# Gate projections moved from the merge stage into the stick-breaking heads of a hybrid decoder layer

## The chip, the cores and the metric

The kernel runs on all 8 cores of one Trainium2 chip. Each core computes one of the 8 batch entries, with no exchange between cores. The metric is the time on the device of the slowest core, in microseconds (us). Engines: PE is the matrix engine (TensorE), DVE VectorE, ACT ScalarE, POOL GpSimd, SP the engine that only issues DMAs here.

## The reference

One decoder layer for x of 2048 tokens by 2048 channels per core. A token mixer (two kinds of attention side by side, 8 heads of 128 each) and a SwiGLU follow one another, each between RMS norms.

```python
u = rms_norm(x)
q_sb,k_sb,v_sb, q_fx,k_fx,v_fx, f_logit, g_sb, g_fx = split(u @ w_in)     # g_*: 2048 columns each
# stick-breaking head: z = q k^T / sqrt(128), strictly causal (s < t)
#   w[t,s] = sigmoid(z_ts) * prod_{s<j<t} (1 - sigmoid(z_tj));   o = w v
# forgetting (fox) head: softmax of z + c[t] - c[s], c = cumulative log sigmoid(f_logit), s <= t
merged = sigmoid(g_sb) * (o_sb @ w_branch_sb) + sigmoid(g_fx) * (o_fx @ w_branch_fox)
h   = x + rms_norm(merged @ w_out)
out = h + rms_norm(swiglu(rms_norm(h)))                                   # d_ff = 5632
```

## The kernel before

Everything is held transposed: channels (or head dimensions) on the 128 partitions, tokens along the free axis. A matmul has 128x128 weights (bf16) and up to 512 token columns. D = 2048 gives KC = 16 channel tiles; the 2048 tokens are NCH = 4 chunks of 512, or two halves of TH = 1024. Weights lie in memory as float32.

The kernel writes a list of instructions for each engine (`KB.op`, `KB.group`, `KB.dma`) and waits between engines come from the buffers that each operation reads and writes. Every engine runs its list in order, so the order in which the Python code emits the work is the order of execution. All compute operations have line 83 in the profile, that of the replay; the tile names tell them apart.

**Front.** x is loaded twice in 16 tiles of 128 x 2048 float32 through two buffers `xs`. The first pass squares each tile on ACT and sums over channels by matmuls with ones (`sq`); `rstd_from_banks` (L362) makes 1/rms by Ln and Exp on ACT. The second pass scales each tile on DVE into `uT` (bf16, the normed input, kept in SBUF). `stage2` (L402) computes the forget logits and the bias tables of the fox heads. Then q, k and v of head 0 are projected.

**Heads.** The 8 stick-breaking heads run first, then the 8 fox heads. While head i runs, the projections of head i+1 run beside it: `head_filler` (L679) makes 24 items of 8 matmuls each (`proj_items`, L484: for each token chunk k, q, v in two halves), and `Filler.tick` emits them evenly over the head's own work. Weights of head i+2 are loaded by SP as float32 (`wst`) and cast on DVE to `wbf` (`load_head`, L463). A finished projection is moved from PSUM by DVE: q and k by a scaled copy, v by a copy into `VT` and a DMA transpose on SP.

`attn_sb` (L597) takes 16 rows of 128 queries, in 24 pieces of up to 1024 keys: logits on PE, `filler.tick`, two sigmoids on ACT (`kap`, `bet`), masks by POOL, a running product (scan) and a product on DVE, then a DMA transpose of the weights on SP into `WTA` or `WTB`. The logits use two pairs of PSUM banks, so piece g+2 waits for the sigmoids of piece g. The value matmuls of a chunk (`pv`, L643) are emitted later: `Steps` is a planner that counts nominal time (`HEAD_US` = 57 us a head) and emits deferred work when its due time has come, here 8 us after the chunk's last piece.

`attn_fox` (L704) takes 40 blocks of 128 keys by 512 queries: logits on PE, `filler.tick`, Exp on ACT into one of 6 buffers `p`, mask on POOL for diagonal blocks, the sum of p on DVE (`acc`), value matmuls 2.7 nominal us later. At the end of a chunk `finish_chunk` (L746) splits the sum into two bf16 parts, adds up over partitions on PE, takes a reciprocal on DVE and multiplies. Each head's output goes to DRAM (`OTs`) through SP.

**Merge.** `P5` (L903) runs once for each half of the tokens. It loads the outputs of all 16 heads (`OTh`, 4 MB) and then, for each of 16 column tiles c, three weight tiles (two gates and the branch weights, float32 by SP, cast by DVE), and computes per 512 tokens 16 + 16 gate matmuls on `uT` and 8 + 8 branch matmuls on `OTh`:

```python
kb.op(ACT, "activation", dict(out=a1.t[:, :], in_=bset[0][0][:, :], func=AF.Sigmoid), ...)
kb.op(DVE, "tensor_tensor", dict(out=m1.t[:, :], in0=bset[2][0][:, :], in1=a1.t[:, :], op=ALU.mult), ...)
kb.op(POOL, "tensor_tensor", dict(out=merged.t[:, c, hsl], in0=m1.t[:, :], in1=m2.t[:, :], op=ALU.add), ...)
```

`WOUT` (L973) follows each half with the output projection. After that come the second norm and the SwiGLU (`GATEUP`, `DOWN`), whose weights POOL loads with a cast to bf16 on the way.

Of the kernel before, what the change touches and what calls it, by code (L numbers as in the profile page):

```python
# [7 lines left out]
F32 = mybir.dt.float32  # L8
# [5 lines left out]
S = 2048  # L14
# [74 lines left out]
class KB:  # L89
# [156 lines left out]
def build_nc(debug=None, upto=99):  # L246
# [16 lines left out]
    G["OTs"] = nc.dram_tensor("OTs", [2 * NH, DH, S], BF16).ap()  # L263
    G["mixs"] = nc.dram_tensor("mixs", [D, S], F32).ap()
# [42 lines left out]
def _emit(nc, kb, banks, G, upto):  # L307
# [5 lines left out]
    gains_d, bf_d, cbf_d, cf_d, outT = G["gains_d"], G["bf_d"], G["cbf_d"], G["cf_d"], G["outT"]  # L313
    OTs, mixs, hs, ffs, dbg = G["OTs"], G["mixs"], G["hs"], G["ffs"], G["dbg"]
# [33 lines left out]
    pre = Slot(kb, "pre", [128, 136], F32)
    cumL = Slot(kb, "cumL", [128, 128], F32)
# [38 lines left out]
    rstd_from_banks([0, 1, 2, 3], rstd1.t, rstd1.r, 0, tmp)
    for c in range(KC):
        x = xs[c % 2]  # L390
        kb.dma(SP, x.ds, x.t[:, :], xT[c * 128:(c + 1) * 128, :], writes=[x.r])
        kb.op(DVE, "scalar_tensor_tensor", dict(out=uT.t[:, c, :], in0=x.t[:, :], scalar=gains.t[:, c:c + 1],
                                                in1=rstd1.t[:, :], op0=ALU.mult, op1=ALU.mult),
              reads=[x.r, gains.r, rstd1.r], writes=[uT.r])
    dump("rstd1", rstd1.t[:, :], rstd1.r)
    if dbg is not None and "uT" in dbg:
        dump("uT", uT.t[:, :, :], uT.r, dbg["uT"].rearrange("(c p) t -> p c t", p=128))
# [825 lines left out]
```

How the kernel before makes its waits and increments, by code:

```python
    def replay(self, eng):  # L70
        regs = {}
        for it in self.prog:
            if it[0] == "w":
                eng.wait_ge(it[1], it[2])
            else:
                _, calls, sem, inc = it
                ins = None
                for meth, kw in calls:
                    if meth == "affine_select":
                        if kw["fill"] not in regs:
                            regs[kw["fill"]] = eng.to_reg(kw["fill"])
                        kw = dict(kw, fill=regs[kw["fill"]])
                    ins = getattr(eng, meth)(**kw)
                    if inc == 16:
                        ins.then_inc(sem, 16)
                if inc == 1:
                    ins.then_inc(sem, 1)
```

## Time and profile before

| | |
|---|---|
| median of 3 runs | 4568.84 us (4557.34, 4568.84, 4719.97) |
| profiled execution | 4541.18 us |
| span of its slowest core (core 5) | 4539.6 us; others 4505.8 to 4533.7 |
| busy share of the span | PE 85%, DVE 35%, ACT 21%, POOL 16% |
| chain that ended last | PE 69%, DMA 11%, DVE 10%, issue 4%, ACT 3%, POOL 2% |
| bytes moved by DMA | 595 MB, mean 131 GB/s |

All rows are from core 5. Times count from the start of its span. "Busy" PE counts matmuls with modelled ends, so a busy PE need not run at its peak; the count of matmuls in a stretch says more. PEclk is the share of full clock that was granted (1.00 is 2.4 GHz, 0.50 is 1.2 GHz). The idle time of an engine is put down to what ended it (`<-`).

### The profile page before, as it was taken

Reading aid. Unit: us, or ns where it says so; the run is one execution under the profiler, and the core shown is the slowest. Engines: PE = TensorE matmul, PEld = TensorE weight load, DVE = VectorE, ACT = ScalarE, POOL = GpSimd, SP = SyncE. Lnnn points to the kernel's source line nnn. Section 1 sums busy time; section 2 is a strip of 40 time slices with the busy share of each in tenths; the row PEclk is TensorE's granted clock in tenths of the full one; section 3 lists DMA queues with packets and bytes.
Section 4 is the critical chain, followed back from the end, with each engine's and each line's share of the span. In section 5 each row is a group of like instructions: output and inputs, shape, how many; then the busy total and the mean of one; then the engine's idle time right before and its main releaser. Section 6 shows DMA issues by size and latency. Waiting matters only on the chain.

```text
span 4539.6 us, 52571 instructions; the slowest of 8 cores (4505.8 to 4539.6 us)
## 1 busy us (share of the span) xinstructions
PE 3868.3 (85%) x17500; PEld 1709.3 (38%) x17500; DVE 1601.8 (35%) x1822; ACT 942.2 (21%) x1421; POOL 725.1 (16%) x933
## 2 busy tenths in 40 slices
PE   2477777779895999989976699998998999999994
PEld 0232333334341444434432244443444444444431
DVE  1478888877776333123322211111100111110001
ACT  3044444434333111211123011111111000000100
POOL 0022222211111111011123011111000111110113
PEclk9998988999997999999998899999999999998886
DMA  6444444321111443654368655565754666558897
GB/s 225 134 102 101 95 109 102 95 75 54 67 45 60 166 150 121 212 185 156 151 215 256 144 117 118 119 121 100 157 114 89 122 120 121 110 114 155 163 197 192
DMA packets 331515, 595.40 MB, mean 131 GB/s; under 512 B 197616, under 2 KB 206320, under 8 KB 298480
## 3 DMA queue, kind: packets, MB, share of 16 engines
q1 hardware_dynamic: 270320, 363.40, 28.7%
q0 software_dynamic: 42496, 195.06, 21.4%
q10 hardware_dynamic: 18432, 33.56, 2.2%
q8 instruction: 145, 2.38, 0.2%
q14 instruction: 122, 1.00, 0.1%
HBM read 633.86 MB, written 75.50 MB: 156 GB/s over the span
## 4 chain that ended last, share of the span: by engine, by line
PE 69%; DMA 11%; DVE 10%; issue 4%; ACT 3%; POOL 2%; DVEq 0%; SPq 0%; ACTq 0%; POOLq 0%
PE ps L83 69%; DVE Pr_43_85 L83 2%; DVE Pr_44_86 L83 2%; DMA mh_106_148<-mixs 2%; DMA xs_23_65<-xT 1%; DMA WTA_47<-wp_45_87 1%; DMA wd_175_217<-wfd_t 1%; ACT kap_39_81 L83 1%; DVE acc_55_97 L83 1%; DMA fl_186_228<-ffs 1%; DVE rec_59_101 L83 1%; DMA xs_22_64<-xT 1%; DMA hs<-hst_108_150 1%; DMA hl_131_173<-hs 0%; DVE uT_49 L83 0%
## 5 line engine op out<-in xcount | busy, mean ns | idle before, releaser
L83 DVE TENSOR_TENSOR_SCAN Pr_43_85<-kap_39_81 128x640 f32<-128x640 f32 (+4 forms) x96 | 160.0, 1667 | 2.2 <-POOL kap_39_81 L83 1.4
L83 PE MATMUL ps<-uT_49,wbf_1_11_53 128*128 128x512 bf16 x512 | 129.7, 402 | 32.2 <-DVE wbf_1_11_53 L83 18.5
L83 PE MATMUL ps<-u_124_166,wgu_0_143_185 128*128 128x512 bf16 x480 | 109.9, 382 | 52.4 <-DVE u_124_166 L83 52.4
L83 PE MATMUL ps<-uT_49,wbf_1_14_56 128*128 128x512 bf16 x512 | 128.1, 397 | 12.7 <-DVE qT_28_70 L83 8.4
L83 POOL TENSOR_SCALAR_AFFINE_SELECT kap_39_81<-kap_39_81 128x128 f32<-128x128 f32 x96 | 45.8, 477 | 581.9 <-ACT kap_39_81 L83 581.1
L83 PE MATMUL ps<-uT_49,wbf_2_12_54 128*128 128x512 bf16 x512 | 123.5, 386 | 15.7 <-DVE kT_29_71 L83 15.5
L83 DVE TENSOR_SCALAR tmpD_169<-ps 128x512 f32<-128x512 f32 x6 | 4.1, 689 | 372.0 <-PE ps L83 366.8
L83 PE MATMUL ps<-uT_49,wbf_0_13_55 128*128 128x512 bf16 x512 | 133.7, 410 | 1.5 <-DVE Pr_44_86 L83 1.5
L83 PE MATMUL ps<-aT_167,wd_153_195 128*128 128x512 bf16 x528 | 120.1, 389 | 14.4 <-DMA wd_153_195<-wfd_t 14.4
L83 PE MATMUL ps<-uT_49,wbf_0_10_52 128*128 128x512 bf16 x512 | 129.7, 402 | 1.1 <-DVE Pr_44_86 L83 1.0
L83 POOL TENSOR_TENSOR merged_104<-m_102_144,m_103_145 128x512 bf16<-128x512 f32 x32 | 63.7, 1990 | 418.1 <-DVE m_103_145 L83 418.1
L83 PE MATMUL ps<-aT_167,wd_175_217 128*128 128x512 bf16 x484 | 120.6, 415 | 8.7 <-DMA wd_175_217<-wfd_t 8.7
L83 PE MATMUL ps<-uT_49,wbf_2_15_57 128*128 128x512 bf16 x512 | 122.2, 382 | 6.0 <-DVE kT_32_74 L83 5.8
L83 DVE TENSOR_TENSOR aT_167<-ps,sg_174_216 128x512 bf16<-128x512 f32 x44 | 30.4, 691 | 273.5 <-PE ps L83 273.5
L83 DVE TENSOR_TENSOR aT_167<-ps,sg_150_192 128x512 bf16<-128x512 f32 x44 | 30.4, 691 | 272.5 <-PE ps L83 272.5
L83 DVE TENSOR_TENSOR aT_167<-ps,sg_173_215 128x512 bf16<-128x512 f32 x44 | 30.4, 691 | 263.6 <-PE ps L83 263.6
L83 DVE TENSOR_TENSOR aT_167<-ps,sg_149_191 128x512 bf16<-128x512 f32 x44 | 30.4, 691 | 262.6 <-PE ps L83 262.6
L83 PE MATMUL ps<-u_124_166,wgu_0_167_209 128*128 128x512 bf16 x480 | 110.4, 384 | 10.1 <-DMA wgu_0_167_209<-wfg_t 10.1
L83 DVE TENSOR_TENSOR_SCAN Pr_44_86<-kap_40_82,Pr_44_86 128x512 f32<-128x512 f32 (+3 forms) x64 | 116.3, 1818 | 7.2 <-DVE Pr_44_86 L83 0.5
L83 PE MATMUL ps<-aT_167,wd_176_218 128*128 128x512 bf16 x484 | 116.3, 404 | 1.3 <-DMA wd_176_218<-wfd_t 1.3
L83 PE MATMUL ps<-aT_167,wd_177_219 128*128 128x512 bf16 x440 | 111.0, 419 | 7.2 <-DMA wd_177_219<-wfd_t 7.2
L83 POOL TENSOR_TENSOR merged_104<-m_76_118,m_77_119 128x512 bf16<-128x512 f32 x32 | 63.5, 1986 | 305.4 <-DVE m_77_119 L83 305.4
(396 smaller groups left out, 7211.6 us busy)
## 6 DMA issues: line engine op xcount, KB each, us to landing
wst_8_50<-wqkv_t SPq DMA_DIRECT2D x24, 1024.0 KB, 6.0
wst_9_51<-wqkv_t SPq DMA_DIRECT2D x24, 1024.0 KB, 6.2
xs_22_64<-xT SPq DMA_DIRECT2D x16, 1024.0 KB, 5.7
xs_23_65<-xT SPq DMA_DIRECT2D x16, 1024.0 KB, 5.9
wstA_64_106<-wg_t SPq DMA_DIRECT2D x16, 1024.0 KB, 5.9
wstA_65_107<-wg_t SPq DMA_DIRECT2D x16, 1024.0 KB, 6.1
wstA_90_132<-wg_t SPq DMA_DIRECT2D x16, 1024.0 KB, 6.3
wstA_91_133<-wg_t SPq DMA_DIRECT2D x16, 1024.0 KB, 6.2
```

Source lines behind the costliest of these rows:

```text
L83: ins = getattr(eng, meth)(**kw)
```

## The change

1. Fox heads run first, stick-breaking heads last. `HEAD_US` is split into `FOX_US` = 58 and `SB_US` = 107, the planner's times.
2. The gate projections leave `P5`. They become 256 filler items of 8 matmuls beside the stick-breaking heads; ACT applies the sigmoid from PSUM and SP stores the result as float32 in DRAM (`gts`, 16.8 MB). `P5` reads it back (1 MB a column tile) and keeps only the branch matmuls.
3. x is loaded once, by token chunk. Each chunk is squared, summed, scaled and projected for the first head before the next is finished.
4. Weights of heads, gates and branches are loaded by POOL with a cast on the way; the float32 buffers and the DVE casts go.
5. q, k and v are moved from PSUM by ACT. In the fox heads the reciprocal on DVE becomes Ln and Exp on ACT; there are 10 `p` buffers, value matmuls come after 4.3 us, the split after 4.3 and the denominator after 8.

```diff
+    def group(self, E, calls, reads=(), writes=(), part=()):      # part: writes without a wait on the own engine
-            kb.dma(SP, sl.ds, sl.t[:, :, :], wqkv_t[br * 24 + j * 8 + h], writes=[sl.r])
-            kb.op(DVE, "tensor_copy", dict(out=dst.t[:, :, :], in_=sl.t[:, :, :]), reads=[sl.r], writes=[dst.r])
+            kb.dma(POOL, sl.ds, sl.t[:, :, :], wqkv_t[br * 24 + j * 8 + h], reads=after, writes=[sl.r])
...
-                kb.op(DVE, "tensor_scalar", dict(out=o_, in0=bt[:, :], scalar1=sc, scalar2=None, op0=ALU.mult),
+                kb.op(ACT, "activation", dict(out=o_, in_=bt[:, :], func=AF.Copy, scale=sc), writes=[br_, dres[tc]])
-                kb.op(DVE, "tensor_copy", dict(out=o_, in_=bt[:, :]), writes=[br_, vt.r])
+                kb.op(ACT, "activation", dict(out=o_, in_=bt[:, :], func=AF.Copy), writes=[br_, vt.r])
...
+    for tc in range(2):
+        for g in range(4):
+            x_load(tc, g)                                          # SP: 4 channel tiles x 512 tokens, 1 MB
+    for ld in load_head(heads[0], 0, after=[xr[0][1]]):
+        ld()
+    for ld in load_head(heads[1], 1, after=[xr[1][3]]):
+        ld()
+    for g in range(4):
+        x_sq(0, g)                                                 # ACT
+        x_stat(0, g)                                               # PE, 4 matmuls
+    x_norm(0)                                                      # rstd, 16 scalings of 512 on DVE, x_load(tc + 2)
+    for g in range(4):
+        x_sq(1, g)
+    for tc in range(NCH):
+        items = proj_items(heads[0], 0, 0, tcs=[tc])
+        for it in items[0:2]:                                      # k
+            it()
+        if tc + 1 < NCH:
+            for g in range(4):
+                x_stat(tc + 1, g)
+            x_norm(tc + 1)
+        if tc + 2 < NCH:
+            for g in range(4):
+                x_sq(tc + 2, g)
+        forget_logits(tc)
+        if tc + 1 == NCH:
+            forget_bias()
+        for it in items[2:]:                                       # q, v
+            it()
...
-            steps.after(2.7, pvm)
+            steps.after(4.3, pvm)
...
-                kb.op(DVE, "reciprocal", dict(out=rc.t[:, :], in_=bD[:, :]), writes=[rD, rc.r])
+                kb.op(ACT, "activation", dict(out=rc.t[:, :], in_=bD[:, :], func=AF.Ln), writes=[rD, rc.r])
+                kb.op(ACT, "activation", dict(out=rc.t[:, :], in_=rc.t[:, :], func=AF.Exp, scale=-1.0), writes=[rc.r])
...
-            steps.after(4.0, dmm)
+            steps.after(8.0, dmm)
...
+    def gate_load(n):
+        sl = wgt[n % 3]
+        kb.dma(POOL, sl.ds, sl.t[:, :, :], wg_t[n], writes=[sl.r])
+    def gate_items(n):                                             # load of n + 2 goes with the first item
+        wsl = wgt[n % 3]
+        def evict_at(tc):
+            def evict(bt, br_):
+                st_ = gst[cnt["g"] % 3]
+                cnt["g"] += 1
+                kb.op(ACT, "activation", dict(out=st_.t[:, :], in_=bt[:, :], func=AF.Sigmoid), writes=[br_, st_.r])
+                steps.after(1.5, lambda: kb.dma(SP, st_.ds, gts[n, :, tc * 512:(tc + 1) * 512], st_.t[:, :],
+                                                reads=[st_.r], writes=[gt_res[n]]))
+            return evict
+        items = []
+        for tc in range(NCH):
+            items += proj_mm(wsl, tc, evict_at(tc))
...
+    def head_filler(i, total, extra=()):                           # projections and gates by turns, 2 items each
...
+    for i in range(NH):
+        filler = head_filler(i, FXW)
+        attn_fox(heads[i], i % 2, filler)
+        filler.flush()
+    steps.drain()
...
+    tot = len(gates) + (NH - 1) * 24
+    for i in range(NH, 2 * NH):
+        want = tot // NH // 2 * 2 - (24 if i + 1 < 2 * NH else 0)
+        ext, gates = (gates[:want], gates[want:]) if i + 1 < 2 * NH else (gates, [])
+        filler = head_filler(i, SBW, ext)
         attn_sb(heads[i], i % 2, filler)
...
     def P5(hf, merged):
+        def fillA(c):
+            sl = wbs[c % 3]
+            kb.dma(POOL, sl.ds, sl.t[:, :, :], wb_t[c], writes=[sl.r])
+        def fillG(c):
+            g = gb[c % 2]
+            kb.dma_multi(SP, g.ds, [(g.t[:, j, :], gts[KC * j + c, :, t0:t0 + TH]) for j in range(2)],
+                         reads=[gt_res[c], gt_res[KC + c]], writes=[g.r])
+        fillA(0)
+        fillA(1)
+        fillG(0)
         for c in range(KC):
+            if c + 2 < KC:
+                fillA(c + 2)
+                fillG(c + 1)                                       # if c + 1 < KC
-                for (bt, br_), wsl in ((bset[0], wgs), (bset[1], wgf)):
-                    kb.group(PE, [("matmul", dict(out=bt[:, :], lhsT=wsl.t[:, k, :], rhs=uT.t[:, k, tsl], ...
-                kb.op(ACT, "activation", dict(out=a1.t[:, :], in_=bset[0][0][:, :], func=AF.Sigmoid),
+                for j, m in enumerate((a, b)):
+                    kb.op(DVE, "tensor_tensor", dict(out=m.t[:, :], in0=bset[j][0][:, :], in1=g.t[:, j, hsl],
+                                                     op=ALU.mult), reads=[g.r], writes=[bset[j][1], m.r])
```

## Rows read from the trace of the kernel before

**Rows 1.** The page: busy tenths of PE and DVE in 40 equal slices.
```profile
PE   2477777779895999989976699998998999999994
DVE  1478888877776333123322211111100111110001
```

**Rows 2.** Windows, start:end and length, busy us (count), then clock, DMA share, GB/s.
```profile
0.00:235.60 235.60, 83.88 (x516) 34.63 (x517) 66.41 (x91) 37.37 (x27) 0.29 (x5) 0.98 0.53 173
235.60:932.30 696.70, 513.97 (x2202) 216.76 (x2201) 600.65 (x600) 298.84 (x385) 166.03 (x256) 0.89 0.42 100
932.30:1392.00 459.70, 416.05 (x1957) 188.41 (x1956) 349.14 (x440) 180.29 (x307) 55.22 (x111) 0.99 0.18 58
...
1451.00:1478.20 27.20, 0.00 (x0) 0.00 (x0) 4.93 (x3) 0.00 (x0) 0.00 (x0) 0.50 0.68 236
1478.20:1820.70 342.50, 334.53 (x1536) 150.87 (x1536) 115.00 (x112) 39.50 (x65) 63.54 (x32) 0.98 0.45 148
...
1960.50:2308.00 347.50, 339.68 (x1553) 153.00 (x1554) 116.25 (x113) 39.50 (x65) 63.69 (x32) 0.98 0.40 151
2320.00:2440.00 120.00, 92.03 (x377) 38.76 (x376) 29.12 (x33) 37.28 (x63) 47.83 (x43) 0.91 0.90 280
2600.00:2700.00 100.00, 100.00 (x465) 45.31 (x464) 13.67 (x20) 11.51 (x19) 16.67 (x24) 1.00 0.57 114
```

**Rows 3.** Waits of PE in the stick-breaking heads: us in total, times, longest.
```profile
PE ps L83 <- ACT bet_41_83 L83: 63.1, 37, 3.4
PE ps L83 <- ACT bet_42_84 L83: 58.9, 31, 4.9
```

**Rows 4.** Groups of instructions in these heads: count, busy us, mean ns, idle before.
```profile
L83 DVE TENSOR_TENSOR_SCAN Pr_43_85<-kap_39_81 128x896 f32<-128x896 f32 x24 | 48.3, 2014 | 0.0
...
L83 ACT ACTIVATE kap_39_81<-ps 128x896 f32<-128x896 f32 x24 | 22.0, 918 | 32.2 <-DVE Pr_43_85 L83 19.6 <-PE ps L83 7.1 <-POOL bet_42_84 L83 5.6
...
L83 DVE TENSOR_SCALAR kT_29_71<-ps 128x512 bf16<-128x512 f32 x16 | 10.9, 682 | 0.0
```

**Rows 5.** Waits of PE in the first seven fox heads.
```profile
PE ps L83 <- DVE acclo_99 L83: 31.4, 12, 3.4
```

**Rows 6.** Groups of instructions in the first seven fox heads.
```profile
L83 DVE RECIPROCAL rec_58_100<-ps 128x512 f32<-128x512 f32 x14 | 46.9, 3351 | 2.3 <-PE ps L83 2.3
...
L83 DVE CAST wbf_0_10_52<-wst_8_50 128x2048 bf16<-128x2048 f32 x3 | 3.7, 1220 | 0.0
```

**Rows 7.** Timeline of ACT at the start: start, us, instruction, idle before.
```profile
11.35 1.28 ACT L83 ACT_TABLE_LOAD   x1 [11.35 <-DMA xs_22_64<-xT]
```

**Rows 8.** Groups of instructions in the first 160 us.
```profile
L83 DVE SCALAR_TENSOR_TENSOR uT_49<-xs_22_64,gains_45,rstd_26_68 128x2048 bf16<-128x2048 f32 x8 | 18.8, 2352 | 16.3 <-DMA xs_22_64<-xT 14.8 <-ACT rstd_26_68 L83 1.6
...
L83 ACT ACTIVATE sq_24_66<-xs_22_64 128x2048 bf16<-128x2048 f32 x8 | 15.3, 1909 | 14.1 <-DMA xs_22_64<-xT 12.0 <-PE ps L83 2.1
...
L83 PE MATMUL ps<-wfb_59,uT_49 128*128 128x8 bf16 x256 | 7.1, 168 | 73.6 <-DVE wfb_59 L83 73.1 <-issue 0.5
...
L83 ACT ACTIVATE tmp_27_69<-tmp_27_69 128x512 f32<-128x512 f32 x4 | 2.5, 629 | 4.3 <-DVE tmp_27_69 L83 4.3
```

**Rows 9.** Groups of the whole run: a scaling of 512 columns on DVE.
```profile
L83 DVE SCALAR_TENSOR_TENSOR hst_108_150<-mh_106_148,gains_45,rstdm_103 128x512 f32<-128x512 f32 x16 | 12.0, 752 | 73.2 <-DMA mh_106_148<-mixs 33.4 <-DMA hs<-hst_108_150 20.1 <-ACT sqm_120_162 L83 9.0
```

**Rows 10.** Timeline of PE: last value matmuls of stick-breaking, first matmuls of P5.
```profile
927.31 5.14 PE L83 MATMUL ps<-WTB_80,V_33_75 128*128 128x512 bf16 x16 [14.61 <-DMA WTB_80<-wp_47_89]
...
1478.25 6.46 PE L83 MATMUL ps<-uT_49,wgA_0_66_108 128*128 128x512 bf16 x16 [27.70 <-DVE wgA_0_66_108 L83]
```

**Rows 11.** The page's DMA issues: engine, count, KB each, median us to landing.
```profile
OTh_105<-OTs SPq DMA_DIRECT2D x1, 4096.0 KB, 16.4
```

**Rows 12.** The tile view of a gate-up weight buffer, loaded by POOL with a cast.
```profile
DMA to landing us min/median/max: 7.0/8.5/10.6
```

**Rows 13.** The tile view of one of the three transposed weight buffers.
```profile
L83 SPq DMA_TRANSPOSE WTA_47<-wp_45_87 x32: 1151/1202/2732, 239.2 to 892.6; - x32
...
DMA to landing us min/median/max: 2.3/2.7/9.6
```

More of the change, by code:

```diff
@@ L388, in _emit @@
[L388 to L395, printed above, removed]
@@ new lines, in x_sq, with x_stat @@
+    def x_sq(tc, g):
+        q = sq[g]
+        kb.op(ACT, "activation", dict(out=q.t[:, :, :], in_=xs[tc % 2].t[:, 4 * g:4 * g + 4, :], func=AF.Square),
+              reads=[xr[tc % 2][g]], writes=[q.r])
+    def x_stat(tc, g):
+        q = sq[g]
+        bt, br = banks[2 + tc % 2]
+        kb.group(PE, [("matmul", dict(out=bt[:, :], lhsT=ones_bf, rhs=q.t[:, j, :], start=(g + j == 0),
+                                      stop=(g == 3 and j == 3))) for j in range(4)],
+                 reads=[q.r, cbf.r], writes=[br])
@@ new lines, in x_norm @@
+    def x_norm(tc):
+        rd = rstd1[tc % 2]
+        rstd_from_banks([2 + tc % 2], rd.t, rd.r, 0, tmp)
+        for k in range(KC):
+            kb.op(DVE, "scalar_tensor_tensor", dict(out=uT.t[:, k, tc * 512:(tc + 1) * 512],
+                                                    in0=xs[tc % 2].t[:, k, :], scalar=gains.t[:, k:k + 1],
+                                                    in1=rd.t[:, :], op0=ALU.mult, op1=ALU.mult),
+                  reads=[xr[tc % 2][k // 4], gains.r, rd.r], part=[ur[tc]])
+            if k % 4 == 3 and tc + 2 < NCH:
+                x_load(tc + 2, k // 4)
@@ L539, in store_O @@
+    for sl in tmp_slots:
+        al.kill(sl.r)
+    al.release(m_h)
+    al.top = m_q1
+    make_qkv(1)
+    assert al.top <= m_h
+    al.top = m_h
     def store_O(hh, c, ost):
@@ new lines, in _emit @@
+    gt_res = [Res(f"gt{n}") for n in range(NGT)]
+    def head_filler(i, total, extra=()):
+        items = proj_items(heads[i + 1], (i + 1) % 2, (i + 1) % 2) if i + 1 < len(heads) else []
+        if i + 2 < len(heads):
+            for x, ld in enumerate(load_head(heads[i + 2], i % 2)):
+                items[2 * x] = (lambda a=items[2 * x], ld=ld: (ld(), a()))
+        if extra:
+            n1, n2 = len(items), len(extra)
+            mix, a, b = [], 0, 0
+            while a < n1 or b < n2:
+                if b >= n2 or (a < n1 and a * n2 <= b * n1):
+                    mix += items[a:a + 2]
+                    a += 2
+                else:
+                    mix += extra[b:b + 2]
+                    b += 2
+            items = mix
+        return Filler(items, total)
@@ L775, in _emit @@
-    for i in range(NH, 2 * NH):
-        filler = head_filler(i, FXW)
-        attn_fox(heads[i], i % 2, filler)
-        filler.flush()
-    steps.drain()
     al.kill(WTA.r)
```

497 lines of the change are left out of this document (230 added, 267 removed).

## The prediction

> **What bounds the kernel now.** I read the 40 slices of the page first [rows 1]. In slices 3 to 8 PE is at 7 tenths and DVE at 8: the stick-breaking heads. After them PE is at 9 or more for most of the run, so a change there must remove matmuls or their waits. Then I cut the run at its stage limits [rows 2]: front (both norm passes, forget gates, projections of head 0) 235.6 us; eight stick-breaking (SB) heads 696.7, or 87.1 each; fox heads 518.7 (to 1451.0; seven with a projection beside them take 459.7, or 65.7 each); a gap of 27.2; P5 first half 342.5, second half 347.5. In SB, DVE is busy 600.7 of 696.7 and PE 514.0, though PE was granted only 0.89 of its clock, and PE waits 122 us for ScalarE's second sigmoid [rows 3], which itself waits for DVE to free its buffers. So SB is DVE's, and P5, where 1536 matmuls fill 334.5 of 342.5, is PE's. A dense PE does 465 matmuls of 512 columns in 100 us [rows 2], 0.215 us each, at a granted clock of 1.00 (2.4 GHz). The sum is made against the profiled execution, 4541.2 us; the median of the runs, 4568.8, stands 0.6% above it, the fastest, 4557.3, 0.36%.
>
> **Front: 235.6 becomes about 123.** The first x tile is there at 11.35 with two in flight [rows 7]; the other two of chunk 0 follow at the fastest rate shown, 280 GB/s [rows 2], 3.75 us each: 19. Then the square 1.9, four statistic matmuls on a cold PE 1.6 (16 after a long wait took 6.46 [rows 10]), the rstd 2.3 (a DVE step like the eviction of [rows 4], two ScalarE steps of 0.63 [rows 8], hops), and 16 scalings of 512 columns. Those aren't in the old front: a quarter of its 2048-column one is 0.59 [rows 8], the same operation at 512 columns into float32 took 0.75 [rows 9]. I take 0.75, its shape: 12.0, so 37. PE runs k of chunk n ahead of the statistic of chunk n+1, so each further chunk costs 6.5 + 1.6 + 2.3 + 12.0 = 22.4: 104. Then k of chunk 3 (6.5), the last forget logits (64 of the 256 that took 7.1 [rows 8]: 1.8), the wait for its short bias chain 3 (an estimate), q and v 32 x 0.215: 123. Ends: 105 (short scalings, warm PE) and 145 (x slowed by 6 MB of head weights, which are now loaded from POOL's queue, where they wait for x tiles and nothing is behind them). Gain 112.
>
> **Fox heads: 8 x 60 = 480 instead of 519.** DVE loses 12 evictions of 0.69, 3 casts of 1.22 and 4 reciprocals of 3.35 [rows 4, 6]: from 349.1/7 = 49.9 us a head to about 25. ScalarE gains 12 evictions and 8 Ln and Exp, 0.63 each [rows 8]: from 25.8 to 38. PE has 192 projection matmuls, 68 full-width equivalents of logits and values, and 8 for the denominator: 268 x 0.215 = 57.7. The 31 us that PE waits for the denominator's low half [rows 5] go, since it is now issued 8 us later. The eviction now stands ahead of the next exponential on ScalarE and can delay it by one filler of 1.7 us; ten p buffers and a value matmul 4.3 us later cover that. I take 60; ends 57.8 and today's 65.7. All eight heads now carry a projection. To SB I add 10 for the drain, a table load and the first gate tiles; ends 3 and 20.
>
> **SB heads: 894 instead of 697.** The gate work is 32 weight tiles x 4 chunks x 16 = 2048 matmuls. The filler has 52 items of 8 matmuls in seven heads and 60 in the last. PE per head: 416 x 0.215 = 89.5, logits and values 14.6, small tiles 2: 106; the last 120. DVE loses 12 evictions and 3 casts: 75.1 - 11.8 = 63. ScalarE has 37.4 of sigmoids and about 27 evictions: 54. So PE becomes the bound. The logits' two bank pairs give ScalarE a whole filler (some 4 us) for eviction and two sigmoids (0.6 + 2 x 0.92 [rows 4]), so the waits of [rows 3] mostly go. What is late next is the value product: its last transpose is issued after about 6 of filler, 2.5 of ScalarE, 3 of DVE (the scan 2.0 [rows 4], the product half of that), 1.2 of SP, and lands 2.7 later [rows 13]: some 15, when PE reaches it at 15 to 18 by the planner's times (in the first chunk 10 against 12). I charge 4 a head: 110 x 7 + 124 = 894. SP gets 16 to 30 gate stores a head, each queued ahead of the piece's transposes but waiting for an eviction that ScalarE does before that piece's sigmoids. POOL issues 7 weight loads a head, ahead of masks of the next piece; they land in 8.5 us [rows 12], and gates are fetched two tiles (27 us of filler) ahead. Ends: 862, and 1046 if the 22.8 us a head stay in which PE is idle today (182.7 in the eight [rows 2]).
>
> **The gap: 27 becomes 43.** SB is now last, and its end is longer: PE waited 14.6 us for the last transpose and took 5.1 for the values [rows 10]; then copy and store 3 (an estimate), the load of all heads' outputs 16.4 [rows 11], and 4 for sharing with weights and gates. Ends 35 and 50.
>
> **P5: twice 345 becomes 129 and 133.** Per column of 128 outputs PE keeps 32 of 96 matmuls: 6.9 us. Now 1 MB of weights (float32, cast in flight) and 1 MB of gates must come in that time. A casting load costs the queues nearly its read bytes: share 0.57 at 114 GB/s in the gate-up stage, where it has 76 of them, against 0.90 at 280 without casts [rows 2]. So the column asks for 1.05 + 0.93 x 1.05 = 2.03 MB, 7.3 us at 280 GB/s. POOL has two sums of 2.0 a column (63.5 for 32 [rows 2]) and one load to issue, less than 6.9. 16 x 7.3 + 4 + the 8 of the first output weights (unchanged) = 129; the second half has 4 more, because all its loads start together. Ends per column 6.9 and 8.6. The Trainium skill, "DMA: Bandwidth & Descriptors", Specifications, states about 358 GB/s of HBM per core: by it a column would be bound by PE, and both halves together 13 us shorter; the most this trace moved is 280.
>
> Sum: start of P5 123 + 480 + 10 + 894 + 43 = 1550 instead of 1478.2 (+72); P5 -213 and -215. Net -356: 4185, and a run 0.36% above it: **4200 us**. With all lower ends 4104, with all upper ends 4479.
>
> **Rivals.** (1) PE stops at each value product: transposes, sharing queues with stores and weights, land like today's slowest, 9.6 instead of 2.7 [rows 13]. For it: no slack. Against: those slow ones stood behind weight loads on SP's queue, which leave it. 32 x 5 = +160: 4360. (2) P5 is bound by loads at 9 us a column (both gate buffers late): 32 x 1.7 = +54: 4254. (3) The clock in SB stays at today's 0.89, because small waits keep lowering it: 894/0.89, +110: 4310. Against: 0.99 in fox, where PE is as dense as SB will be. (4) The gates aren't hidden: DVE's and ScalarE's dependences keep their 87.1 a head and the fillers come on top, 28 x 1.72 = 48: 135 a head, 1082, +188: 4388. The change then only moves the work. (5) All attention runs on a clock lowered by a limit common to the die, since PE is then dense on eight cores for 1.4 ms more. It decides from a granted clock of 0.83 over fox and SB: 1374 x (1/0.83 - 1) = +281, 4481, no change that can be told; today SB has 0.89 [rows 2], with an idle PE. Against: 1.00 in the gate-up stage and 0.98 in P5, both dense. The Trainium skill, "TensorE: Matmul & The Clock Gate", Part 1, states such a limit, 13/16 once three cores of a die run dense matmuls (by it +317, 4517); the trace doesn't show it in its dense stages. (6) Slower: ScalarE and PE alternate. Since the filler's eviction is queued ahead of the piece's sigmoids, each logits matmul finds its bank taken until eviction and both sigmoids are done: 0.6 + 1.8 [rows 4, 8] + 0.5 of hops = 2.9 us for each of 192 pieces, +557: 4757, and slower than before from 1.9 us a piece. Against: two bank pairs, and the filler of the piece between is longer than 2.9 in all but the first chunk.
>
> **Chances.** Forecast 0.58; (1) 0.12; (2) 0.08; (3) 0.07; (4) 0.07; (5) 0.04; (6) 0.04. A measurement here tells about 2% from no change. Faster: the forecast and (1) to (4), 0.92; same (5), 0.04; slower (6), 0.04. Range 4100 to 4390: from the lower ends to rival (4); it leaves out (5), (6), part of (1) and (4), and the forecast's tail above, under 0.2.
>
> **What would show it.** First fox logits at 115 to 130 us; fox heads at 60 with no wait for the low half; SB heads at 106 to 112 with PE clock 0.97 or more, DVE near 0.58 and PE waits for ScalarE below 5 us a head; P5 halves at 117 to 125 of matmuls with DMA share near 0.9. The prediction fails if SB heads take over 122, or if PE's waits in SB name transposes or ScalarE for more than 15 us a head.

## The result, and the profile after

The changed kernel takes 4174 to 4190 us in the runs that are compared, against 4557 to 4569 before: a ratio of 0.917 (95% interval 0.9135 to 0.9204), faster by 8.3%. The profiled execution took 4189.8 us, its slowest core 4188.2. In some executions of every kernel here, old or new, some of the cores are granted a lower clock for much of the time (0.81 where a trace shows it); their times are left out of all comparisons, which leaves two experiments (e1, e4) with a single run and one (e8) with none.

The first reading is again the 40 slices of the page, now of the changed kernel. Against [rows 1] the hole in PE's row at slices 3 to 8 is gone; what is left lies at the front, at three places in the middle (the starts of the two P5 halves, and the second output projection with the second norm) and at the end.

```profile
PE   5999999999999969977639999989999999999973
DVE  3444445656566523122131111111001111110001
PEclk8999999999999989989869999999999999999987
```

Then the stages, cut at their first matmuls, in the columns of [rows 2]: front; fox heads; stick-breaking (SB) heads; gap; P5 first half; output projection; P5 second half; second output projection with the second norm.

```profile
0.00:135.20 135.20, 77.49 (x517) 35.14 (x518) 53.31 (x117) 42.95 (x38) 4.60 (x12) 0.80 0.61 158
135.20:611.70 476.50, 464.78 (x2242) 215.72 (x2240) 220.52 (x364) 280.51 (x511) 73.54 (x155) 1.00 0.25 44
611.70:1490.40 878.70, 853.98 (x4041) 391.84 (x4039) 521.28 (x478) 403.25 (x596) 196.85 (x303) 0.99 0.61 117
1490.40:1533.00 42.60, 5.26 (x17) 1.99 (x18) 4.27 (x3) 2.53 (x3) 1.60 (x3) 0.57 0.69 171
1533.00:1656.60 123.60, 113.42 (x512) 50.05 (x513) 43.00 (x65) 0.00 (x0) 47.05 (x45) 0.97 0.88 207
1656.60:1802.10 145.50, 119.43 (x544) 53.55 (x544) 19.79 (x17) 42.01 (x69) 1.62 (x3) 0.91 0.70 201
1802.10:1922.40 120.30, 113.00 (x513) 50.61 (x514) 44.30 (x65) 0.00 (x0) 47.01 (x45) 0.97 0.88 211
1922.40:2194.10 271.70, 149.03 (x577) 60.57 (x578) 67.97 (x83) 61.10 (x104) 73.13 (x70) 0.80 0.86 221
```

PE is busy in 97.5% of the fox stretch and 97.2% of the SB stretch. The waits that are left to PE there, of the changed kernel (us, times, longest), answer to [rows 3] and [rows 5]. In SB:

```profile
PE ps L83 <- DMA WTA_95<-wp_62_104: 12.8, 4, 5.2
PE ps L83 <- ACT bet_58_100 L83: 8.4, 7, 1.2
PE ps L83 <- DMA WTA_95<-wp_61_103: 2.4, 2, 1.2
PE ps L83 <- DMA WTB_96<-wp_61_103: 1.1, 1, 1.1
```

and in the fox heads:

```profile
PE ps L83 <- DVE Ost_17_59 L83: 7.9, 7, 1.1
PE ps L83 <- DVE acclo_92 L83: 2.3, 1, 2.3
PE ps L83 <- POOL p_45_87 L83: 1.4, 1, 1.4
```

The 122 us of waiting for ScalarE's second sigmoid have become 8.4, the 31 us for the denominator's low half 2.3.

Where the 351 us went, from span to span: front -100.4; first logits to P5 +155.2; P5 first half -218.9; output projection +5.7; P5 second half -221.5 (the old window of [rows 2] ran 5.7 us into the next stage; its first output matmul is at 2302.3); second output projection and norm +38.1; the rest -9.6. The +38.1 is in code that didn't change. The row of the kernel before for that stretch, in the same columns:

```profile
2302.30:2535.90 233.60, 140.28 (x576) 59.15 (x576) 67.99 (x83) 63.21 (x105) 73.18 (x70) 0.83 0.89 257
```

Counts agree to within two with the last row of the changed kernel, and DVE's and POOL's busy times to 0.1 us. What differs is the rate of the DMAs, 257 GB/s before and 221 now, and PE's granted clock, 0.83 and 0.80.

### The profile page after: what moved, and what is told of

Same layout as the page of the kernel before. It is cut to its first block, busy times and chain, and to the rows that moved or that the text cites. A ratio compares the mean times of both kernels' runs of the same rounds, so it can differ in the third digit from the quotient of the medians.

```text
span 4188.2 us, 52026 instructions; the slowest of 8 cores (4130.2 to 4188.2 us)
## 1 busy us (share of the span) xinstructions
PE 3764.6 (90%) x17500; PEld 1699.2 (41%) x17500; DVE 1191.8 (28%) x1501; ACT 1046.4 (25%) x1673; POOL 737.3 (18%) x1046
## 3 DMA queue, kind: packets, MB, share of 16 engines
HBM read 617.09 MB, written 109.05 MB: 173 GB/s over the span
## 4 chain that ended last, share of the span: by engine, by line
PE 78%; DMA 15%; DVE 2%; issue 2%; POOL 2%; ACT 1%; SPq 0%; DVEq 0%; ACTq 0%; POOLq 0%
PE ps L83 78%; DMA fl_185_227<-ffs 3%; DMA hs<-hst_109_151 3%; DMA xs_21_63<-xT 1%; DMA wd_175_217<-wfd_t 1%; POOL hst_109_151 L83 1%; DMA WTA_95<-wp_62_104 1%; DVE uT_48 L83 1%; DMA mh_107_149<-mixs 1%; DMA hl_133_175<-hs 1%; DMA OTh_136<-OTs 1%; DMA OTh_115<-OTs 1%; DMA WTA_95<-wp_61_103 1%; DMA wd_177_219<-wfd_t 0%; DMA mh_106_148<-mixs 0%
## 5 line engine op out<-in xcount | busy, mean ns | idle before, releaser
L83 PE MATMUL ps<-u_124_166,wgu_0_143_185 128*128 128x512 bf16 x480 | 111.1, 385 | 56.3 <-DVE u_124_166 L83 56.3
L83 PE MATMUL ps<-uT_48,wgt_64_106 128*128 128x512 bf16 x704 | 160.5, 379 | 0.0
L83 PE MATMUL ps<-uT_48,wgt_65_107 128*128 128x512 bf16 x704 | 160.0, 379 | 0.0
L83 PE MATMUL ps<-uT_48,wbf_1_8_50 128*128 128x512 bf16 x512 | 128.1, 399 | 34.0 <-DVE uT_48 L83 23.1
L83 PE MATMUL ps<-uT_48,wgt_66_108 128*128 128x512 bf16 x640 | 145.6, 379 | 0.0
L83 PE MATMUL ps<-aT_167,wd_175_217 128*128 128x512 bf16 x484 | 116.3, 404 | 19.9 <-DMA wd_175_217<-wfd_t 19.9
L83 PE MATMUL ps<-aT_167,wd_153_195 128*128 128x512 bf16 x528 | 117.0, 382 | 13.3 <-DMA wd_153_195<-wfd_t 13.3
L83 PE MATMUL ps<-uT_48,wbf_0_7_49 128*128 128x512 bf16 x512 | 121.4, 385 | 0.0
L83 PE MATMUL ps<-uT_48,wbf_1_11_53 128*128 128x512 bf16 x512 | 121.3, 383 | 0.0
L83 PE MATMUL ps<-uT_48,wbf_2_12_54 128*128 128x512 bf16 x512 | 119.6, 379 | 0.0
L83 PE MATMUL ps<-uT_48,wbf_2_9_51 128*128 128x512 bf16 x512 | 119.3, 379 | 0.0
L83 PE MATMUL ps<-uT_48,wbf_0_10_52 128*128 128x512 bf16 x512 | 119.0, 379 | 0.0
L83 PE MATMUL ps<-u_124_166,wgu_0_167_209 128*128 128x512 bf16 x480 | 109.9, 382 | 9.9 <-DMA wgu_0_167_209<-wfg_t 9.9
L83 PE MATMUL ps<-aT_167,wd_176_218 128*128 128x512 bf16 x484 | 107.7, 382 | 6.8 <-DMA wd_176_218<-wfd_t 6.8
L83 PE MATMUL ps<-aT_167,wd_177_219 128*128 128x512 bf16 x440 | 100.9, 391 | 12.8 <-DMA wd_177_219<-wfd_t 12.7
L83 PE MATMUL ps<-u_124_166,wgu_1_170_212 128*128 128x512 bf16 x480 | 108.5, 379 | 0.0
L83 PE MATMUL ps<-u_124_166,wgu_1_168_210 128*128 128x512 bf16 x480 | 108.5, 379 | 0.0
L83 PE MATMUL ps<-u_124_166,wgu_0_169_211 128*128 128x512 bf16 x480 | 108.5, 379 | 0.0
L83 PE MATMUL ps<-u_124_166,wgu_1_144_186 128*128 128x512 bf16 x480 | 108.5, 379 | 0.0
```

The source lines that it names most:

```text
L83: ins = getattr(eng, meth)(**kw)
```

## The experiments

Ratios are to the kernel before, with 95% intervals. Single times are the runs that are compared. The kernel before took 4557 to 4569 us beside the changed kernel and 4529 to 4598 beside the experiments (middle runs 4537 to 4548), so a difference in us between the changed kernel and an experiment carries some 20 us of that; a difference of ratios doesn't.

**1. Squares behind the evictions (e1).** In the front, ScalarE's work for chunk n+2 is moved:

```diff
-        if tc + 2 < NCH:
-            for g in range(4):
-                x_sq(tc + 2, g)
         forget_logits(tc)
 ...
         for it in items[2:]:
             it()
+        if tc + 2 < NCH:
+            for g in range(4):
+                x_sq(tc + 2, g)
```

> The squares of chunk n+2 are issued on ScalarE behind the evictions of q and v of chunk n instead of ahead of them; nothing else changes. Theory (ScalarE's in-order queue made the front's extra 12 us: the k projection of chunk 1 waited 10.9 us for q's eviction, which stood behind squares that wait for x): k of chunk 1 starts at about 64 instead of 69.9, the first fox logits come at 126 to 129 instead of 135.2, and the whole run is 6 to 9 us shorter (0.2%). Rival (x's loads, 16 to 20 us each under load, set the front whoever waits for them): the wait only moves to the statistic matmuls, first logits at 133 to 136, no gain.

In the changed kernel's timeline (start, us, instruction, idle before and what ended it) ScalarE waits for x with two squares, and only then evicts q of chunk 0, whose matmuls ended at 55.5; PE's k projection of chunk 1 waits for that bank:

```profile
63.91 1.91 ACT L83 ACTIVATE sq_25_67<-xs_21_63 128x2048 bf16<-128x2048 f32 x1 [7.58 <-DMA xs_21_63<-xT]
67.39 1.91 ACT L83 ACTIVATE sq_26_68<-xs_21_63 128x2048 bf16<-128x2048 f32 x1 [1.57 <-DMA xs_21_63<-xT]
69.21 0.58 ACT L83 ACTIVATE qT_18_60<-ps 128x512 bf16<-128x512 f32 x1
69.93 5.07 PE L83 MATMUL ps<-uT_48,wbf_1_8_50 128*128 128x512 bf16 x16 [10.93 <-ACT qT_18_60 L83]
```

In the experiment (core 4 too) the eviction comes first and the same matmuls wait for DVE's scaling alone:

```profile
55.12 0.60 ACT L83 ACTIVATE qT<-ps 128x512 bf16<-128x512 f32 x1 [2.91 <-PE ps L83]
63.26 6.20 PE L83 MATMUL ps<-uT,wbf 128*128 128x512 bf16 x16 [4.78 <-DVE uT L83]
66.63 1.91 ACT L83 ACTIVATE sq<-xs 128x2048 bf16<-128x2048 f32 x1 [1.26 <-DMA xs<-xT]
```

First fox logits at 126 to 128 us on the six cores with a full clock, 127.6 on core 4 (135.2 before the move); the one run that is compared took 4153.6 us, which is too few to tell 8 us by. In the front the theory holds: 7.6 us are ScalarE's order. That x still lands at 66.6 shows why it isn't the whole 10.9.

**2. Gates back in P5 (e2).** Everything else of the change stays:

```diff
-    gates = []
-    for n in range(NGT):
-        gates += gate_items(n)
 ...
+                    kb.group(PE, [("matmul", dict(out=bt[:, :], lhsT=wgA[c % 3][j].t[:, k, :],
+                                                  rhs=uT.t[:, k, t0 + tc * 512:t0 + (tc + 1) * 512],
 ...
+                    kb.op(ACT, "activation", dict(out=s_.t[:, :], in_=bset[2 + j][0][:, :], func=AF.Sigmoid),
```

> The gate projections go back into P5 (weights by POOL with a cast, three buffers, sigmoids on ScalarE, four banks as before); the stick-breaking (SB) heads keep everything else, with the old planner time of 57; no gates go through DRAM. P5 should take about 342 a half again (+219 and +222 us). Theory A (without gates the SB heads fall to what DVE needs, 65 us busy a head, plus hops): 70 to 75 us a head, SB about 590 instead of 891, so the kernel at about 4189 - 300 + 441 = 4330. Theory B (the round trip PE, ScalarE, DVE sets an SB head, not DVE's busy time, and the evictions moved to ScalarE don't help): about 85 a head, SB 690, kernel at about 4430. Either way the stretch from the second output projection to the first gate-up matmul, 246 to 277 us on the cores of the changed kernel, 232 to 248 before: if the gates' DRAM traffic just ahead of it or their fetch makes it longer, it is back at about 240; if it is chance between cores, or where tensors lie in DRAM (the gates' tensor is still declared), it stays near 255.

Measured: 4311 to 4326 us, ratio 0.950 (0.9455 to 0.9549). The window from the first SB logits to the end of the SB matmuls but for the last value product, core 6:

```profile
607.50:1195.00 587.50, 454.49 (x1953) 194.16 (x1991) 519.02 (x480) 339.25 (x471) 187.18 (x274) 0.88 0.47 90
```

From 627 to 1230 us, a window that ends behind the last value product, PE waits for

```profile
PE ps L83 <- ACT bet L83: 100.9, 77, 3.5
PE ps L83 <- DMA WTB<-wp: 31.5, 6, 26.6
```

The longest wait of the second line, 26.6, is that of the last value product, which lies outside the window above. The last logits end at 1182.8: 575 us, 72 a head, DVE busy 0.88 of the window, PE at a granted clock of 0.88, near the old 0.89 of [rows 2], and with its old kind of wait for ScalarE, whose sigmoids wait 93 us for DVE. Theory A holds. One number of it was missed: P5's halves took 371 to 376 and 355 to 367 us on the eight cores, not about 342, since each now has a wait for the outputs in it (32.8 and 24.2 us on core 6). The gain splits in two: hiding the gates is worth about 135 us by the middle runs (4321 against 4186) and about 150 by the ratios (0.950 against 0.917), all the rest of the change 220 to 225 (4542 to 4321, or 1 to 0.950). SB heads had fallen from 87 to 72 before any gate was moved in; that this is DVE's loss of evictions and casts fits its busy share, but no run without the gates takes one of the two back alone. The stretch from the second output projection to the first gate-up matmul took 248 to 259 us here, mean 254, with no gate traffic at all: the gates are not what made it long.

**3. Evictions on VectorE again (e3).**

```diff
-                kb.op(ACT, "activation", dict(out=o_, in_=bt[:, :], func=AF.Copy, scale=sc), ...)
+                kb.op(DVE, "tensor_scalar", dict(out=o_, in0=bt[:, :], scalar1=sc, scalar2=None, op0=ALU.mult), ...)
```

(and v by a copy likewise)

> The changed kernel with the evictions of q, k and v on VectorE again (front, fox and SB); the gates' sigmoids stay on ScalarE. Theory (PE bounds both kinds of heads now, and DVE at 59% in SB and 46% in fox has room for 12 x 0.69 = 8 us a head): SB 110 to 112 a head, fox 59 to 61, the whole within 0.5% of the changed kernel, so the engine of the evictions is worth next to nothing once the gates fill PE. Rival (an eviction waits behind a scan of up to 2 us on DVE and holds one of the two filler banks): PE waits for DVE some 5 us a head in SB and 2 in fox, +50 to +60 us (1.3%).

Measured: 4161 to 4165 us, ratio 0.9159 (0.9138 to 0.918), so 10 to 29 us less than the changed kernel by the times and 5 by the ratios: no difference that can be told. Windows of fox and SB heads, core 3:

```profile
140.00:600.00 460.00, 457.02 (x2205) 212.61 (x2203) 272.54 (x448) 234.56 (x408) 69.11 (x146) 1.00 0.26 45
630.00:1480.00 850.00, 827.79 (x3921) 380.07 (x3922) 556.78 (x546) 342.48 (x491) 179.62 (x286) 0.99 0.60 116
```

PE is as full as with ScalarE's evictions. First fox logits come at 127 to 131, against 132 to 135: that is the front of experiment 1 by another way, as the evictions leave the queue with the squares. Beside gates that fill PE, the engine of the evictions is worth nothing; the 15 us a head that SB had lost in experiment 2 are, as I read the two together, the same slack, and can be spent once.

**4. The old finish of the fox heads (e4), and with VectorE's evictions (e6).**

```diff
-            steps.after(4.3, pvm)
+            steps.after(2.7, pvm)
 ...
-            steps.after(4.3, split)
+            split()
 ...
-                kb.op(ACT, "activation", dict(out=rc.t[:, :], in_=bD[:, :], func=AF.Ln), writes=[rD, rc.r])
-                kb.op(ACT, "activation", dict(out=rc.t[:, :], in_=rc.t[:, :], func=AF.Exp, scale=-1.0), writes=[rc.r])
+                kb.op(DVE, "reciprocal", dict(out=rc.t[:, :], in_=bD[:, :]), writes=[rD, rc.r])
 ...
-            steps.after(8.0, dmm)
+            steps.after(4.0, dmm)
```

(and six p buffers instead of ten)

> The changed kernel with the fox heads' old finish: reciprocal on VectorE (3.35 us), split at once, denominator matmuls after 4.0 and value matmuls after 2.7 planner us, six p buffers. Evictions stay on ScalarE. Theory (the late denominator took away PE's 4.5 us a head of waiting for the low half, and the early value matmuls wait for the exponential once evictions stand ahead of it): fox 62 to 64 a head instead of 59.5, +20 to +36 us. Rival (DVE's evictions were what made the low half late; without them the old finish is as good): fox under 60.5 a head, less than +8 us.

Measured: 4274.5 us, one run. From first fox logits to first SB value product, which took 495 or 496 us on the cores of the changed kernel, it took 607 to 613: 14 us a head, three to six times the theory's price, and the rival is far off. PE's waits, core 3:

```profile
PE ps L83 <- POOL p L83: 60.3, 40, 2.1
PE ps L83 <- ACT p L83: 24.5, 24, 1.0
PE ps L83 <- DVE acclo L83: 21.1, 8, 3.2
```

The low half is the 21 us that I had expected. The other 85 are value matmuls that wait for an exponential or the mask behind it, which points to the 2.7; the six buffers and the reciprocal changed with it, and no run takes them apart. e6 puts the evictions on DVE besides:

> The run with the fox heads' old finish (reciprocal on VectorE, matmuls after 2.7 and 4.0, six p buffers: it took 73 a head) and, besides, the evictions of q, k and v on VectorE again: fox heads as before the change, but for the casts of weights. Theory (an interaction: an eviction on ScalarE stands ahead of the exponential, and value matmuls issued only 2.7 later then wait for it and for POOL's mask; on VectorE it doesn't): fox 60 to 65 a head, PE waits for p below 2 us a head, about 70 us less than that run. Rival (the old delays or the reciprocal alone cost 14 us a head, whoever evicts): fox stays at 71 to 75.

Measured: 4199 and 4221 us, ratio 0.9227 (0.907 to 0.9384); the same stretch takes 525 to 537. PE's waits, core 0:

```profile
PE ps L83 <- DVE acclo L83: 24.1, 8, 3.3
PE ps L83 <- ACT p L83: 3.9, 8, 0.6
```

So it is the interaction: an eviction ahead of the exponential costs 78 us (609 to 531) with the old finish, whose value matmuls are issued 2.7 later, and nothing (495 against 498 in e3) with the new one, where they are issued 4.3 later. The new finish is worth 114 us with ScalarE's evictions, 33 with VectorE's (531 against 498).

**5. SB heads first (e5).** The two loops change places, with the gates still in the SB heads.

```diff
-    heads = list(range(NH, 2 * NH)) + list(range(NH))
+    heads = list(range(2 * NH))
```

> The changed kernel with the stick-breaking (SB) heads first again: gates still fill the SB heads (each now carries the next head's projection too, 448 filler matmuls), the last fox head runs without a filler. Theory (the order only moves work): SB 8 x 112 = 896, fox 7 x 59.5 = 417 and a last head of 40 to 59 on ScalarE and VectorE alone, a gap of 27 instead of 30 before P5: within 15 us of the changed kernel, 4165 to 4200. Rival (SB heads at the front run as they did in the old kernel, with a granted clock near 0.89 and PE waiting for ScalarE): SB over 950, the kernel above 4240.

Measured: 4189 to 4194 us, ratio 0.9186 (0.9087 to 0.9285), within the theory's numbers: the order only moves work. In the profiled execution the SB heads took 914 to 921 us on six cores, but 949 and 953 on cores 6 and 7, the two that ended last: their granted clock was 0.83 up to 300 us, with PE busy 162 of those 168 us, where core 4 had 1.00.

**6. Outputs early (e7), with bfloat16 gates (e8), with one column (e11); bfloat16 gates alone (e9).** P5's first matmuls wait 28.7 and 24.4 us for the 4 MB of outputs (changed kernel, timeline of PE):

```profile
1532.99 9.14 PE L83 MATMUL ps<-OTh_115,wb_74_116 128*128 128x512 bf16 x32 [28.66 <-DMA OTh_115<-OTs]
1802.13 4.43 PE L83 MATMUL ps<-OTh_136,wb_95_137 128*128 128x512 bf16 x10 [24.35 <-DMA OTh_136<-OTs]
```

The core of e7's edit:

```diff
+        def load0(n_, hh):           # beside the last SB head's filler items
+            free()
+            OTs0[hh] = at(off0[n_], f"OT0_{n_}", [128, TH], BF16, dma=True)
+            ot_load(hh, 0, OTs0)
 ...
+    p5a = P5(0, merged, wout_pre)
+    for _ in range(2):
+        next(p5a)
+    steps.drain()
 ...
+    WOUT(0, merged, nofill, each=lambda c: ot_load(heads[c], 1, OTs1))
```

> The changed kernel with the squares behind the evictions, and SBUF laid out so that the loads around P5 start early: the heads' outputs of the first half are loaded head by head beside the last SB head (into weight and q, k, v buffers that are no longer used), those of the second half beside the first output projection (into the dead normalised input), the first weight of P5 and of each output projection ahead of its stage, and the first two columns of P5 are issued ahead of the last value product. Theory (PE stands idle 29 and 24 us for the outputs, 7 each for the first output weights, and some 9 at the last value product): 60 to 80 us less than the run with the squares moved, 4075 to 4095. Rival (P5 is bound by loads, DMA share 0.88, and the traffic moved beside other stages makes SB's transposes and the output projection late): less than 40 us, above 4110.

Measured: 4152 to 4164 us, ratio 0.9105 (0.896 to 0.9251), no better than the 4153.6 (one run) of the squares alone. The theory is wrong, and the rival right in the first half of P5, on four cores of eight. Cores 2 to 5 run it dense, cores 0, 1, 6 and 7 don't; the same 70 us of e7 on core 4, then on core 7:

```profile
1530.00:1600.00 70.00, 70.00 (x327) 31.71 (x325) 26.94 (x41) 0.00 (x0) 30.34 (x30) 1.00 0.96 223
...
1530.00:1600.00 70.00, 65.58 (x295) 28.85 (x294) 23.08 (x36) 0.00 (x0) 25.63 (x26) 0.98 0.95 189
```

PE's waits of core 7 from 1490 to 1650:

```profile
PE ps L83 <- DVE m L83: 12.7, 3, 9.2
PE ps L83 <- DMA wb<-wb_t: 9.9, 5, 2.8
PE ps L83 <- POOL merged L83: 8.7, 1, 8.7
```

The DMA engines are busy 0.96 and 0.95 of the time on the two cores. The second half became longer too: 132 to 142 us on six cores (core 7 waits 7.7 us in it for weights and 12.5 for the last sum) and 119 and 122 on cores 5 and 4, where the changed kernel took 120 to 124 on all. As I read it, the old wait for the outputs was also the time in which weights and gates got two columns ahead; without it the loads are the bound where a core gets the lower rate. The 9.2 is a self-made wait: the second early column took the banks of the last value product, and VectorE, which frees them, waited for gates. So gates in half the bytes should pay now, and should not before:

```diff
-    G["gts"] = nc.dram_tensor("gts", [2 * KC, 128, S], F32).ap()
+    G["gts"] = nc.dram_tensor("gts", [2 * KC, 128, S], BF16).ap()
```

(with the store and load buffers in bfloat16 as well, which rounds the gates)

> The kernel before it with the gates kept in DRAM as bfloat16 instead of float32: 67 MB less to move. Theory (a P5 column takes 7.5 to 7.7 us because 2 MB of loads must come in that time, and PE needs 6.9): P5 halves at 112 to 114 us with DMA share near 0.65, 12 to 20 us less than the kernel before it. Rival (P5 is PE's already, its 113 us of matmuls being the whole stage but for the start): less than 5 us.

The 67 MB are wrong: float32 gates are 33.5 MB, written once and read once, and bfloat16 takes away half of those 67. (The list of the change gives 16.8 MB for them; by the two pages the bytes written to memory rise from 75.50 to 109.05 MB.) There is no time to compare. Four cores in each of three runs had a granted clock of 0.95 to 0.97 in the mean; they end at 4072 to 4148, against 4088 to 4163 in e7: the right direction, the size not told.

> The run with the squares moved, and gates kept in bfloat16; all loads at their old places. Theory (with the outputs loaded at the start of P5, PE is dense behind them, 99 of 100 us on two cores of the run with the squares moved, and two columns of gates are there before it begins; loads bound only the slower cores): P5 halves 118 to 121 become 115 to 118, the kernel 4 to 14 us shorter, 4140 to 4150. Rival (P5 is bound by loads all along, its 0.9 of DMA share being all there is): 12 to 20 us shorter, 4134 to 4142.

Measured: 4142, 4146 and 4172 us, ratio 0.9157 (0.911 to 0.9205), P5 halves 119 to 122: no change that can be told from the 4153.6 (one run) of the squares alone. Neither size came. The DMA share in the first half is 0.62 on core 2, where it was 0.90 on core 4 of e1, and the length is the same, 120.5 and 120.3 us: P5 with its old start isn't bound by loads.

> The kernel with early loads and bfloat16 gates, with one column of P5 instead of two ahead of the last value product (the second column's banks made that product wait 8 to 9 us for VectorE, which waited for gates), and the second weight of P5 in a buffer that comes free earlier. Theory (in the run with early loads and float32 gates P5 became bound by its loads, DMA share 0.97 from 1560 to 1640 us on one core, so what the early loads gave was lost there; half the gate bytes give it back): cores end at 4060 to 4120, the slowest at 4095 to 4125, 30 to 60 us under the run with only the squares moved. Rival (the stretch from P5 to the second norm is bound by its bytes as a whole, wherever they are loaded): above 4135.

Measured: 4108 to 4118 us, ratio 0.9062 (0.9032 to 0.9093): below every compared run of e1, e7 and e9, inside the theory's numbers, and below the changed kernel by about 70 us in the times (1.7%) and 50 in the ratios (1.2%). All cores now run P5's first half dense; the slowest, core 0, in its timeline and in a window:

```profile
1527.31 103.76 PE L83 MATMUL ps<-OT,wb 128*128 128x512 bf16 x470
```

```profile
1530.00:1590.00 60.00, 59.74 (x275) 27.20 (x279) 23.85 (x36) 0.00 (x0) 25.50 (x25) 1.00 0.72 157
```

Fifteen columns in 103.8 us are 6.9 each, PE's own time; the DMA share, 0.93 to 0.99 on the cores of e7, is 0.71 to 0.78. So the early loads paid once the bytes were cut and one column instead of two was ahead, with the second weight in another buffer. Which of these did it isn't shown: e8, with the bytes alone, has no time to compare, and no run has one column with float32 gates.

**7. The gates' tensor last in DRAM (e10).**

> The run with the squares moved, with the gates' DRAM tensor declared behind the others, so that the tensors of the mixer, the residual and the feed-forward lie where they lay in the old kernel. The stretch from the second output projection to the first gate-up matmul took 240 us in the mean of eight cores before, 255 in the changed kernel, 254 with the gates back in P5. Theory (where tensors lie in DRAM): back at 237 to 243. Rival (not the place): 246 to 256.

Measured: 4151 and 4162 us, ratio 0.9156 (0.9116 to 0.9195). In the profiled execution, which is neither of these two and took 4419 us, the stretch took 241 to 244 us on cores 0, 1, 6 and 7, and 253 to 258 on cores 2 to 5, which had a granted clock of 0.81 from the fox heads on and came to it 250 us later; the mean is 249. That is within the rival's numbers, but with cores so far apart it settles nothing. Other kernels with this code unchanged gave means of 246 (e3, e4, e9) to 254 (e2) with the tensor at its place, and single cores from 237 to 260; e7 and e11, which load this stage's first weight earlier, gave 240 and 239. So the 272 of the slowest core of the changed kernel is the upper end of a scatter, and 6 to 15 us of the mean over the old 240 stay unexplained.

## Why the prediction was right

The forecast for the profiled execution was 4185, measured 4189.8. The mechanism held: PE became the bound of SB, its idle time there fell from 183 to 25 us with the gates, and P5 lost two thirds of its matmuls. That the sum is 5 us off and not 30 or 40 is luck: 38 us too little in code that didn't change stand against 33 too much elsewhere.

- **What bounds.** SB was DVE's and became PE's: with the gates in, PE is busy 854 of 878.7 us and DVE 521. Without them (e2) DVE, busy 0.88 of the window, is again what ScalarE and through it PE wait for.
- **Front: 123 forecast, 135.2 measured, the step that failed.** It lies outside the 115 to 130 that I had given as a sign. "Each further chunk costs 22.4": VectorE's scalings of the four chunks (start, us) ended at 41.2, 63.5, 91.8 and 114.5, so 22.3, 28.3 and 22.7.

```profile
30.48 10.69 DVE L83 SCALAR_TENSOR_TENSOR uT_48<-xs_21_63,gains_45,rstd_0_27_69 128x512 bf16<-128x512 f32 x16 [1.56 <-ACT rstd_0_27_69 L83]
52.83 10.69 DVE L83 SCALAR_TENSOR_TENSOR uT_48<-xs_22_64,gains_45,rstd_1_28_70 128x512 bf16<-128x512 f32 x16 [1.55 <-ACT rstd_1_28_70 L83]
81.10 10.69 DVE L83 SCALAR_TENSOR_TENSOR uT_48<-xs_21_63,gains_45,rstd_0_27_69 128x512 bf16<-128x512 f32 x16 [1.85 <-ACT rstd_0_27_69 L83]
103.79 10.69 DVE L83 SCALAR_TENSOR_TENSOR uT_48<-xs_22_64,gains_45,rstd_1_28_70 128x512 bf16<-128x512 f32 x16 [1.55 <-ACT rstd_1_28_70 L83]
```

  The 28.3 has the squares ahead of the evictions in it; I had put ScalarE's steps on the path without the order of its queue (e1: 7.6 us). The rest: chunk 0 was ready 4 us later than my 37, since the last x tile landed at 24 and not 19, with the tiles of chunk 1 and head weights in the queues beside it, and the end took 1.7 more. The scaling cost 10.7 a chunk, between my two bounds.
- **Fox: 490 with the change-over forecast, 476.5 measured.** The heads begin 57.3, then 59.1 to 59.3 us apart, where I took 60, and the last one takes 64.1 with the change-over, which I had at 70. "Ten p buffers and a value matmul 4.3 us later cover that" was the step that carried most, and more than I had priced: with the old finish in its place the eviction costs 78 us (e4, e6).
- **SB: 894 forecast, 878.7 measured.** The first seven heads take 108.4 each for my 110, the last 120.1 for 124. Transposes land in 2.3/3.5/9.5 and 2.2/2.9/16.9 us (least, median, most; into the two buffers), slower than [rows 13], yet PE waits for them 16 us in all eight heads, not 4 a head. Rival (1) needed 5 a product, rival (3) a clock of 0.89 where 0.99 was granted, rival (4) 135 a head, and rival (6) 2.9 a piece: PE's waits for ScalarE are 8.4 in 192 pieces.
- **The gap: 43 forecast, 42.6 measured.** 8.7 for the last transpose, 5.3 of values, 28.7 to the landing; the 4 MB took 25.8 instead of 16.4 with weights and gates beside it.
- **P5: 129 and 133 forecast, 123.6 and 120.3 measured.** The step that failed is the 7.3 a column: I had the loads as the bound. PE was busy 113 of each half, 16 columns at its own 6.9 and some more, and half the gate bytes change nothing (e9); with 6.9 the sum for the first half gives 122. What a lead of two columns at the start does for it is argued, not shown. Loads do bound P5 on some cores where the outputs come early (e7): my reason was right at the wrong place. The 280 GB/s was not the most that the old trace moved, either: from 1460 to 1480 us it moved 320. By the Trainium skill, "DMA: Bandwidth & Descriptors", Specifications (about 358 GB/s a core), PE would bound a column, and in the changed kernel it did. In e7 the queues of core 7 were busy 0.95 at 189 GB/s, about 250 by the bytes read (an estimate: a column reads 2.1 MB, of which 1.6 are counted, as a casting load counts by the 512 KB that it writes), so that figure is no guide to what such a stage of casting and plain loads gets.
- **Rival (5), the clock.** Granted 1.00 in fox and 0.99 in SB, with all eight cores dense. The rule in the Trainium skill, "TensorE: Matmul & The Clock Gate", Part 1, that three dense cores of a die lower the clock to 13/16 did not show in this execution. Where a trace has 0.81, which is 13/16, it could go to pairs of cores and not to a whole die: in e10, 0.81 on cores 2 to 5 from 140 to 600 us and 1.00 on cores 0, 1, 6 and 7 (PE busy 456 of those 460 us on core 2, 447 on core 0).
- **Not in the forecast: +38 in unchanged code** on the slowest core, 15 of it in the mean of the eight cores (240 to 255) and the rest the scatter between cores; its cause is open (e10). Without it the forecast would have been some 33 us too high: SB, fox and the two P5 halves were charged 15, 13 and 18 too much and the front 12 too little; the other unchanged stages came 4 shorter; and 6 go off again, since [rows 2] cuts the old second half 5.7 too long.
- **Whose gain it is.** The forecast gave each part a price but not what they share. e2 and e3 together point to it: DVE's relief and the gates use the same idle PE time. Moving the evictions is worth nothing once the gates are in, and the order of the heads nothing either (e5).

## What to carry to other kernels

Work that fills an idle engine is worth the idle time, not the work: price what the stage would take without it first, as other parts of the same change may already have used that slack. When an operation moves to another in-order engine, list what then stands behind it, and what that one waits for; the same move cost nothing, 7.6 or 78 us here by its neighbours. A wait at the start of a stage may be what gives its loads their lead: before you cut the wait, ask whether the loads still come in time without it (e7 gained nothing by cutting it).

## What the runs showed of the hardware that was not expected

In one stage of one execution (e7, 1530 to 1600 us), with DMA shares of 0.93 to 0.99 on all cores, cores 2 to 5 moved 223 to 230 GB/s and cores 0, 1, 6 and 7 only 189 to 195, for the same loads. A load of 4 MB took 25.8 us here, with weights and gates loaded beside it, and 16.4 in the kernel before. And a stretch of unchanged code with the same instructions took 232 to 277 us from core to core and kernel to kernel; at 234 and 272 us it moved 257 and 221 GB/s, with DMA shares of 0.89 and 0.86.
